# One transformer kernel on one core: products that keep the token rows are spread around the place products, and the first pair's gather is cut in two

## The reference

```python
expert_id = (grp[:, None] * EXPERTS_PER_GROUP + top_idx).reshape(-1)
hb = jax.nn.silu(xb @ w_gate[e]) * (xb @ w_up[e])
return (hb @ w_down[e]) * g[:, None]
y = zeros_like(x2).at[slot_tok].add(y_blocks)
h = h + y
```

## Time and profile before

| | |
|---|---|
| median of three runs | 1373.38 us |
| the three runs | 1370.48, 1373.38, 5935.26 us |
| profiled execution | 1371.7 us, of which the span is 1370.0 |
| granted TensorE clock, mean | 0.947 of full speed |
| TensorE busy | 1210.8 us (88% of the span) |
| VectorE, ScalarE, GpSimd busy | 467.8, 269.4, 323.6 us |
| DMA, mean over the span | 245 GB/s, 335.84 MB |

### The profile page before, as it was taken

One profiled execution on the slowest core, in us unless ns is written; L12 is line 12 of the kernel. 1 busy time (PEld: TensorE's weight loads), 2 busy tenths in 40 slices (PEclk: granted clock), 3 DMA queues, 4 the chain that ended last, 5 costly groups with the idle time before them and its releaser, 6 DMA issues.

```text
span 1370.0 us, 18547 instructions
## 1 busy us (share of the span) xinstructions
PE 1210.8 (88%) x7562; PEld 790.6 (58%) x7571; DVE 467.8 (34%) x1160; ACT 269.4 (20%) x687; POOL 323.6 (24%) x343
## 2 busy tenths in 40 slices
PE   8999999886956566666899999999999999999997
PEld 6864556352512122221477559999448666999843
DVE  3443434101001010110214646444573224544467
ACT  4313432010000000000225542111013222111100
POOL 5000100000000000000101347878101113978800
PEclk9999999998978777888999999999999999999999
DMA  9643346999999999999976226544333048544400
GB/s 347 195 175 123 123 179 246 426 427 425 427 428 427 428 429 429 428 426 423 400 250 219 83 75 203 186 172 147 144 133 144 0 152 279 197 149 178 154 1 31
DMA packets 101358, 335.84 MB, mean 245 GB/s; under 512 B 6728, under 2 KB 58240, under 8 KB 87069
## 3 DMA queue, kind: packets, MB, share of 16 engines
q1 hardware_dynamic: 98662, 326.33, 61.9%
q0 software_dynamic: 2416, 8.30, 1.7%
q10 hardware_dynamic: 199, 0.06, 0.0%
HBM read 333.59 MB, written 2.86 MB: 246 GB/s over the span
## 4 chain that ended last, share of the span: by engine, by line
PE 72%; DMA 18%; DVE 3%; POOL 3%; ACT 2%; issue 2%; SPq 1%; POOLq 0%; DVEq 0%; ACTq 0%
PE bank L1708 18%; PE bank L892 17%; DMA ring<-in_w_expert_up 10%; PE bank L1758 8%; PE bank L1248 5%; PE bank L1266 4%; DMA ring<-in_w_expert_down 2%; DMA ring<-in_w_expert_gate 2%; PE bank L1866 2%; DMA wide_rows<-in_w_expert_gate 2%; PE bank L1138 2%; PE bank L1679 2%; PE bank L1527 1%; PE bank L1500 1%; PE bank L1055 1%
## 5 line engine op out<-in xcount | busy, mean ns | idle before, releaser
L892 PE MATMUL bank<-wide_rows,ring 128*128 128x256 f32 (+3 forms) x576 | 126.3, 371 | 0.2 <-ACT ring L2008 0.2
L1708 PE MATMUL bank<-R,arena 128*128 128x128 f32 x1056 | 125.1, 275 | 0.0
L1248 PE MATMUL bank<-ring,arena 128*32 128x512 f32 x512 | 78.4, 702 | 51.2 <-DMA ring<-in_w_expert_up 38.8
L1708 PEld LDWEIGHTS bank<-R,arena 128*128 128x128 f32 x1056 | 121.5, 192 | 0.0
L892 PEld LDWEIGHTS bank<-wide_rows,ring 128*128 128x128 f32 (+1 forms) x576 | 104.3, 189 | 19.5 <-issue 3.9
L3169 POOL COPY arena<-w_router 128x256 f32<-128x256 f32 x1 | 0.4, 396 | 473.3 <-PE bank L1248 473.3
L2685 DVE TENSOR_TENSOR arena<-arena,bank 64x512 f32<-64x512 f32 x16 | 11.1, 692 | 292.8 <-ACT arena L2121 292.8
L1248 PE MATMUL bank<-wide_rows,arena 128*32 128x512 f32 x128 | 67.5, 677 | 45.5 <-DMA arena<-in_w_expert_up 34.0
L1708 PE MATMUL bank<-wide_rows,ring 128*128 128x128 f32 x704 | 91.2, 275 | 1.5 <-ACT wide_rows L2106 1.5
L1708 PEld LDWEIGHTS bank<-wide_rows,ring 128*128 128x128 f32 x704 | 84.7, 192 | 2.5 <-ACT wide_rows L2106 2.5
L1266 PE MATMUL bank<-ring,arena 128*32 128x512 f32 x504 | 71.6, 709 | 13.5 <-ACT arena L2124 10.1
(11 more groups left out here) (389 smaller groups left out, 1978.8 us busy)
## 6 DMA issues: line engine op xcount, KB each, us to landing
ring<-in_w_expert_down SPq DMA_DIRECT2D x29, 2048.0 KB, 16.1
ring<-in_ffn_w_in SPq DMA_DIRECT2D x44, 1024.0 KB, 8.3
ring<-in_w_expert_gate SPq DMA_DIRECT2D x16, 2048.0 KB, 24.8
ring<-in_w_expert_up SPq DMA_DIRECT2D x16, 2048.0 KB, 32.0
arena<-in_w_expert_up SPq DMA_DIRECT2D x14, 2048.0 KB, 32.9
ring<-in_ffn_w_out SPq DMA_DIRECT2D x10, 2048.0 KB, 7.9
ring<-in_w_in SPq DMA_DIRECT2D x7, 2048.0 KB, 15.8
arena<-in_w_expert_gate SPq DMA_DIRECT2D x7, 2048.0 KB, 27.2
```

The lines of the kernel that those rows point to most:

```text
L892: last = pe.matmul(dst, lhsT, rhs, start=k == 0, stop=k == len(pairs) - 1)
L1248: last = pe.matmul(bank[e % 2][at:at + SLOTS, :], xg_tile(e % 2, k)[:, SLOTS * r:SLOTS * r + SLOTS], w[r][:, kk, :], start=k == 0, stop=k ...
L1708: last = pe.matmul(up_banks[layer][u % 4][i][:, at * P:(at + 1) * P], weights(k), columns(k), start=k == 0, stop=k == KT // 2 - 1)
```

## The change

On TensorE two of the four rows products stay ahead of the place products; the third takes the place of the two bf16 products of zeros, and the fourth stands behind the first half of pair 0's gather. The second half of that gather moves behind the first half of gate and up. `gather_pair` now does one half for each call; the gather of pair 1 is done by two calls in a row, as before. On VectorE the take of the second half moves behind the other 30 experts' picks and the gates of the first quad. The computation is the same.

```diff
-            for tb in range(TB):
-                for n in range(2):
-                    last = pe.matmul(bank[4 + 2 * tb + n][:, :], ident[:, :], X[:, tb, n * HALF:(n + 1) * HALF], start=True, stop=False)
-            last.then_inc(x_kept, 1)
+            def rows_kept(tb, n):
+                return pe.matmul(bank[4 + 2 * tb + n][:, :], ident[:, :], X[:, tb, n * HALF:(n + 1) * HALF], start=True, stop=False)
+
+            for n in range(2):
+                rows_kept(0, n)
             pe.wait_ge(gate_ready, 1)
...
-            def gather_pair(r, done):
-
-                for k in range(KT):
+            def gather_pair(r, j):
+
+                for k in range(4 * j, 4 * j + 4):
                     at = (k % 4) * P + r * DUO
-                    last = product(bank[2 + k // 4][:, at:at + DUO],
+                    last = product(bank[2 + j][:, at:at + DUO],
                                    [(R[:, tb, k * P:(k + 1) * P], pick[:, tb, r * DUO:(r + 1) * DUO]) for tb in range(TB)])
-                    if k % 4 == 3:
-                        last.then_inc(done, 1)
+                return last
...
-            keep_awake(2, jobs.bank("pos"))
+            rows_kept(1, 0)
             pe.wait_ge(moe["picks"], 1)
             pe.wait_ge(ffn_rows, 2)
-            gather_pair(0, first_gathered)
+            gather_pair(0, 0).then_inc(first_gathered, 1)
+            rows_kept(1, 1).then_inc(x_kept, 1)
             moe_gate_up(0, 0, 0, first=True)
+            gather_pair(0, 1).then_inc(first_gathered, 1)
             moe_gate_up(0, 1, 0)
             pe.wait_ge(moe["picks"], 2)
-            gather_pair(1, moe["gathered"])
+            for j in range(2):
+                gather_pair(1, j).then_inc(moe["gathered"], 1)
...
-            for j in range(2):
+            def first_take(j):
                 dve.wait_ge(first_gathered, j + 1)
                 take_gathered(j, (0,)).then_inc(first_taken, 1)
+
+            first_take(0)
             picks(slice(2, EXPERTS)).then_inc(moe["picks"], 1)
             dve.wait_ge(moe["picks"], 2)
             gates_of(0).then_inc(moe["gated"], 1)
+            first_take(1)
```

## The result

| | before | after |
|---|---|---|
| median of the runs | 1373.12 us (20 runs) | 1375.29 us (20 runs) |
| lowest, highest | 1370.47, 5935.26 us | 1372.16, 1377.80 us |
| ratio of after to before | | 1.0017, 95% interval 1.0009 to 1.0024 |
| profiled execution, span | 1371.7, 1370.0 us | 1376.55, 1374.8 us |
| granted clock, mean | 0.947 | 0.942 |

The changed kernel is slower by 0.17%, 2.3 us: far within 2%, but outside what the interval leaves open, and in the other direction than forecast. The ratio leaves out the one execution of 5935.26 us, which belongs to a slower state of the machine. Its 20 times fall into two groups with a gap between: eight from 1372.2 to 1373.7 us at a mean clock of 0.947 to 0.949, and twelve from 1374.6 to 1377.8 at 0.942 to 0.946. The profiled execution is one of the twelve.

The account below looks back on a forecast made before the run. Expert weight loads bound the kernel; first half 1.9 us earlier, less 0.4 for a slow start, leaves 1.5: 1370.2 from the profiled 1371.7, 1371.9 from the median, so 1371.0 forecast; range 1368.0 to 1377.0 us.

Parts of the forecast that it names:

- What bounds the kernel: Expert weight loads bound 240 to 685 us; at the change, when TensorE's products let SyncE issue the next loads matters.
- Place products earlier: With two rows products ahead, the place products end at 221.55 instead of 223.10: 1.5 us gained.
- Third rows product: Replacing two bf16 products, it runs from 222.5 to 223.35 at full clock; gather starts 1.0 us earlier.
- open take: VectorE's take of the second gather half, no longer hidden: 0.42 plus two hand-overs, 0.5 us.
- The clock stays low: Rival: half clock outlasts 220.5 by more than about 2 us; kernel 3 us slower, 1374.7 up to 1377; chance 0.32.
- the slack of 2.4: DMA work still queued at the 261.8 issue: 3.3 us, less 0.9 from issue to traffic.
- the other reading: The forecast itself, half clock ending as before: a lead of 1 to 2 us, chance 0.43.
- TensorE's chain alone counts: Rival: no queue slack at 262, so the first half's lead is waste; 1372.1 us, chance 0.13.
- just enough: At 261.8, a stream 1.9 us earlier and an issue 0.35 later use 2.25 us of the slack of 2.4.
- The early issue does nothing: Rival: the later X load fills the DMA hole; if loads only share, 0.5 of lead left, 1371.2 us; chance 0.10.
- one start in place of two: The 3 MB (traffic 230.5) join the X load's traffic ending 230.5; their stream runs 1.9 us ahead.

Follow-up runs that it names:

- number 3: After, plus four bf16 products of zeros behind the first two rows products; 1371.73 us, ratio to before 0.9999.
- number 4: After, but three rows products ahead of the place products and the two zeros products back in the third's place; 1372.14 us, ratio to before 0.9996.
- number 2: Before, with only the rows products spread: two ahead, third replacing the zeros products, fourth behind the whole, uncut gather; 1377.53 us, ratio 1.0036.
- number 1: Before, with only pair 0's gather cut in two halves and VectorE's second take moved; 1372.71 us, ratio 1.0002.
- number 5: After, unchanged, timed once more; 1374.86 us against before at 1372.96, ratio 1.0020.
- number 6: After, plus two bf16 products of zeros behind the place products; 1373.91 us, ratio to before 1.0015.
- number 11: Number 4 unchanged, timed once more; 1373.07 us against before at 1373.06, ratio 1.0003.
- number 7: Before, with four small bias transposes and ScalarE's copy of them moved behind the four rows products; 1372.55 us, ratio 1.0004.
- number 12: Before, plus only three bf16 products of zeros behind the place products; 1373.02 us against before at 1371.89, ratio 1.0003.
- number 8: Number 4 with the edit of number 7 (bias transposes behind the three rows products ahead); 1375.32 us, ratio to before 1.0013.
- number 9: After, plus a bf16 product of zeros behind every second router product, eight in all; 1377.19 us, ratio to before 1.0031.
- number 10: Number 4 plus three bf16 products of zeros behind the place products; 1371.26 us against before at 1373.06, ratio 0.9990.

## Why the prediction was wrong

**What bounds the kernel** held. The change moved the issues, the issues moved the DMA stream, and the stream moved the end; behind 270 us the difference in moved bytes stays.

**The step that failed** is the one under "Place products earlier" and "Third rows product": that the half clock ends at 220.5 with two rows products ahead as with four, and that everything behind takes its time at full clock. In the profile it ended at 231.3. From the third rows product to the end of the second half the forecast has 12.8 us (222.5 to 235.3) and the trace 17.6 (222.74 to 240.35). The 4.8 us more are, by the chain:

| step | forecast | after | number 3, full clock | number 4, full clock |
|---|---|---|---|---|
| third rows product | 0.86 | 2.04 | 1.10 | (ahead) |
| first half of the gather | 1.80 | 3.31 | 1.73 | 1.81 |
| fourth rows product | 0.86 | 1.81 | 0.91 | 0.91 |
| gate and up, first half | 3.50 | 4.27 | 3.57 | 3.57 |
| second half of the gather | 1.80 | 1.94 | 1.94 | 1.94 |
| open take | 0.5 | 0.60 | 0.60 | 0.60 |
| gate and up, second half | 3.50 | 3.64 | 3.64 | 3.64 |

Number 3 has the order of after, at full clock from 219.8 on, and needs 13.5 us for the seven steps. So 4.1 of the 4.8 us are the clock. The other 0.7 is what the forecast had too short at full clock: 0.24 at the third rows product, and 0.05 to 0.14 at each step from the fourth on; in particular the second half of the gather and that of gate and up are each 0.14 longer than half of the whole. The issues forecast for full clock (226.1, 229.6, 235.4, 262.1) came in number 3, behind its four zeros, at 226.60, 230.14, 236.31 and 263.07, up to 1.0 late. Those of number 4 lie within 0.4 us (226.05, 229.59, 235.76, 262.52), which is in part luck, since it does the work in another order. The plan was read rightly in the main but for the clock.

**The rival "The clock stays low" is what happened**, and its numbers held: 2.1 to 4.0 us later for the first half (measured 2.6), 4.4 to 6.3 for the second (5.4), 2.0 to 3.9 at the end of the stage (3.25; the 5.36 of the second half less the slack of 2.4 is 3.0). Within its price, though, the place products were put at 0.8 us more and took 1.3 more (2.36 for 1.05). The median rose by 2.2 us and not by 3 or more, since eight executions of 20 stay at the time of before: the median of those eight is 0.2 us above it, that of the other twelve 3.8. The forecast went by the other reading, with 0.43 to the 0.32 of this one. I had read that the clock came back behind the same work sooner or later, and left it open; I should have asked where in the products the return lay. Before had 1.5 us of rows products still to run when the clock came back at 220.5: the change takes away more than these.

The experiments that undo it settle that the clock is the cause: number 3 puts dense work back in that place and nothing else, and the slowdown is gone; number 4 does the same with a rows product; number 2 has the loss without the cut; number 1 the cut without the loss.

**Why only in some executions.** The profiles differ in when the clock falls within the router's products. Two rows products ahead:

| kernel, profile | router from | clock falls | rows products | clock back |
|---|---|---|---|---|
| number 3 | 210.67 | 212.9 | 216.67 to 220.17 | 219.8 |
| number 2 | 210.51 | 213.1 | 216.25 to 220.02 | 219.9 |
| after | 210.81 | 214.2 | 215.77 to 219.55 | 231.3 |
| number 5 (after) | 212.56 | 215.9 | 217.54 to 221.32 | 233 |
| number 6 | 209.09 | 212.3 | 214.25 to 218.03 | 229.3 |

Where it falls early, the router's last products and the transposes are slow, the rows products start later and still run when it comes back. Where it falls late, 3.2 us or more into the router, they start earlier and have ended. In before and in numbers 1 to 4 and 11 this stretch of half clock lasted 6.8 us; had it lasted as long in the three late ones, it would have ended at 221.0, 222.7 and 219.1 (an estimate), 1.1 to 1.5 us behind their rows products. The place products that ran there in after kept TensorE busy (1.00 in the windows from 220 and 221), and the clock stayed at 0.50. With three ahead the late fall does no harm, as in this row of the timeline of number 11, whose clock fell at 212.7, 3.2 us into its router, and was back at 219.5:

```profile
214.68 5.21 PE L1208 MATMUL bank<-X,ident 128*128 128x512 f32 x6
```

The products still ran at the return. It is a reading of six profiles, not a thing that an experiment set: what decides where in the router the clock falls was not tried, and that the eight executions of the lower group are those with an early fall was not seen. The Trainium skill (TensorE: Matmul & The Clock Gate, Part 1: The HAM clock gate) has sustained activity release the throttled state. The traces agree in direction: in before and in numbers 1 to 4, 7, 11 and 12 the return (at 219.2 to 220.6) came while rows products ran, in number 8 (220.4) 0.1 us behind them. But the same two rows products saw it in numbers 2 and 3 and not in after, which that statement by itself does not tell apart. So the prediction's words, that the trace agrees that the rows products released the clock, said more than one trace could.

**"TensorE's chain alone counts"** was right in part. At full clock the lead of the stream was as large as the issues made it (2.1 us at 255), but the issue at 262.5 let only 1.0 through; the forecast had 1.5 and called the slack "just enough". The second half was 1.0 us later against the router, not 0.35: mis-sized by 0.5 in the pieces, and 0.1 comes from three products ahead instead of two. In the time even that 1.0 us is not to be found (numbers 4 and 11).

**"The early issue does nothing"** did not come: in number 4 the stream led by as much as the issues did. But "one start in place of two" gave nothing either. There the X load still runs when the 3 MB join, as the windows show:

```profile
229.00:230.00 1.00, 1.00 (x13) 0.54 (x5) 0.00 (x0) 0.00 (x0) 0.00 (x0) 1.00 0.99 418
230.00:231.00 1.00, 1.00 (x12) 1.00 (x10) 0.00 (x0) 0.00 (x0) 0.00 (x0) 1.00 1.03 238
231.00:232.00 1.00, 0.46 (x5) 0.33 (x3) 0.50 (x2) 0.00 (x0) 0.00 (x0) 1.00 0.80 238
232.00:233.00 1.00, 0.93 (x12) 0.41 (x16) 0.81 (x6) 0.00 (x0) 0.00 (x0) 1.00 0.85 360
```

The DMA engines are taken to 0.80 and more, and move 238, 238 and 360 GB/s before they reach 483. From an empty queue, in number 1, it was 188, 246 and 410. The slow start was not avoided by joining the loads.

## What to carry to other kernels

Before dense products are moved out of a place, look in narrow windows for the microsecond in which the granted clock returns there, and for how much of them is still to run then: here 1.5 us of 5.7 was all the margin, and the change moved 2.3 us away (5.74 less 3.44 for the two that stay). Products that seem to be only in the way may be what ends the half clock, and where they must go, dense ones that nobody needs (number 3) or one needed product left in place (number 4) kept the time here. And a stream that starts 1.8 us earlier was worth nothing measurable here, where the queue later waits for an issue on TensorE's own chain: that chain would have to be shortened first.

## What the runs showed that was not expected

- The same kernel has two groups of times some 4 us apart (1372.2 to 1373.7 and 1374.6 to 1377.8), seen in two sets of runs. The mean clock goes with them. The border is not sharp: before reaches 1374.64 in the first set, and four of its 35 runs beside numbers 1 to 4 lie above 1374.6, up to 1375.90.
- The clock can fall again 3 to 4 us behind its return, when small products, waits and the gather follow: at 223.3 in number 2 (back at 219.9), 224.0 in number 7 (220.6), 223.8 in number 8 (220.4). In number 9 it fell there, at 223.4, though it had been at 1.00 since 200 us, and in numbers 10 and 11 at 238.5 and 240.0.
- Fp32 gathers lose as much as dense products at half clock: 6.59 and 6.72 us (numbers 2 and 7) for 3.60, half a gather 3.31 for 1.81. I had put 1.5 us on the half, and it was 1.5.
- Where the zeros products stand decides what they buy: behind the place products nothing that can be measured (numbers 6 and 12), among the router's a low stretch elsewhere (number 9), four of them behind the first two rows products the whole slowdown undone (number 3).
- Number 8 had one execution at 1367.98 us, 5 us below the median before. What would bring every execution there stays open, as does what decides when the clock falls within the router's products, and why it was low at 679 us in some profiles.
